# Attention in a diffusion block: ScalarE instead of VectorE makes the rounded high parts of finished pairs and of the keys

## The reference

```python
# latent queries: blocks of 8x16 tokens against a 12x32 neighbourhood and 512 cached tokens
s_lat = einsum(qb, kg) * scale + bias        # relative bias, masked to the 8x16 window
s_ctx = einsum(qb, k_ctx) * scale
p = softmax(concatenate([s_lat, s_ctx], -1))
o = p[..., :n_lat] @ vg + p[..., n_lat:] @ v_ctx
# context queries: blocks of 128 against the 256 context keys
mix = concatenate([o, pool_mixer(u)], -1) @ w_out
```

## Time and profile before

| | |
|---|---|
| median of 3 runs | 4138.67 us (4134.81 to 4142.27) |
| profiled execution | 4139.76 us, span 4138.2 us |
| TensorE busy | 3860.6 us (93%) |
| VectorE busy | 2504.6 us (61%) |
| ScalarE busy | 1815.9 us (44%) |
| GpSimd busy | 502.6 us (12%) |
| from 1120 to 1688 us (attention) | TensorE 523.35, VectorE 392.47, ScalarE 364.50, GpSimd 276.73 of 568 us |

### The profile page before, as it was taken

The page is one execution under the profiler, slowest core; times in us unless marked ns, Lnnn a source line. Parts: engine busy times, 40 slices in busy tenths (PEclk is TensorE's granted clock), DMA queues, the critical chain, the costliest instruction groups (busy, mean ns, idle before and its releaser), DMA issues. The chain is left out here.

```text
span 4138.2 us, 68556 instructions
## 1 busy us (share of the span) xinstructions
PE 3860.6 (93%) x25046; PEld 3388.2 (82%) x25046; DVE 2504.6 (61%) x4812; ACT 1815.9 (44%) x2830; POOL 502.6 (12%) x501
## 2 busy tenths in 40 slices
PE   7999999999799989799997699999999999999992
PEld 3688888888688878799996688888888888888881
DVE  4645555555367777322324677777777777777774
ACT  3611111111266666211104466666666666666652
POOL 0000000000255554000000000000000000000000
PEclk9999999999899999899998799999999999999996
DMA  9434444444555544736316577778777777788776
GB/s 348 152 127 132 137 129 132 132 132 132 151 155 175 159 144 148 252 120 212 128 59 252 168 250 258 255 251 263 252 251 249 252 255 252 257 260 268 250 239 243
DMA packets 572379, 825.46 MB, mean 199 GB/s; under 512 B 23728, under 2 KB 458368, under 8 KB 560512
## 3 DMA queue, kind: packets, MB, share of 16 engines
q1 hardware_dynamic: 548448, 700.96, 52.0%
q0 software_dynamic: 23840, 123.26, 9.2%
HBM read 717.21 MB, written 108.00 MB: 199 GB/s over the span
## 5 line engine op out<-in xcount | busy, mean ns | idle before, releaser
L1959 DVE TENSOR_TENSOR e_wlo<-e_raw,e_whi 128x1024 fp32r<-128x1024 f32 x768 | 905.2, 1219 | 348.9 <-ACT e_whi L1879 345.9
L2091 PE MATMUL ps<-e_xs,e_whi 128*128 128x320 f32 x4096 | 1060.6, 345 | 15.5 <-DVE e_xs L1967 7.9
L2091 PE MATMUL ps<-e_xs,e_wlo 128*128 128x160 f32 x4096 | 934.7, 238 | 0.0
L1879 ACT ACTIVATE e_whi<-e_raw 128x1024 fp32r<-128x1024 f32 x768 | 768.9, 1054 | 326.5 <-DMA e_raw<-in_w_up 109.8
L2091 PEld LDWEIGHTS ps<-e_xs,e_whi 128*128 128x128 f32 x4096 | 754.7, 188 | 24.6 <-DVE e_wlo L1959 11.9
L2091 PEld LDWEIGHTS ps<-e_xs,e_wlo 128*128 128x128 f32 x4096 | 770.3, 191 | 0.7
L2109 PE MATMUL ps<-e_whi,e_h 128*128 128x512 f32 x1024 | 406.2, 397 | 9.2 <-DVE e_h L1993 9.2
L488 PE MATMUL ps<-hhi,p_whi 128*128 128x512 f32 (+1 forms) x1536 | 386.4, 360 | 8.7 <-DVE p_wlo L427 8.7
L445 DVE SCALAR_TENSOR_TENSOR p_acc<-p_modraw,cT,p_acc 128x256 f32<-128x256 f32 x960 | 386.5, 479 | 0.6 <-DMA p_modraw<-in_w_mod 0.6
L488 PE MATMUL ps<-hlo,p_whi 128*128 128x512 f32 (+1 forms) x1536 | 383.4, 358 | 0.0
L488 PE MATMUL ps<-hhi,p_wlo 128*128 128x512 f32 (+1 forms) x1536 | 383.1, 358 | 0.0
(11 more groups left out here) (245 smaller groups left out, 5708.7 us busy)
## 6 DMA issues: line engine op xcount, KB each, us to landing
e_raw<-in_w_gate SPq DMA_DIRECT2D x64, 2048.0 KB
e_raw<-in_w_up SPq DMA_DIRECT2D x64, 2048.0 KB
e_raw<-in_w_down SPq DMA_DIRECT2D x64, 2048.0 KB
p_modraw<-in_w_mod SPq DMA_DIRECT2D x128, 512.0 KB, 3.6
m_raw<-in_w_mod SPq DMA_DIRECT2D x16, 2048.0 KB, 14.8
p_raw<-in_w_in SPq DMA_DIRECT2D x64, 512.0 KB, 4.9
o_raw<-in_w_out SPq DMA_DIRECT2D x16, 2048.0 KB, 8.6
projT<-p_out_st POOLq DMA_DIRECT2D x32, 640.0 KB, 3.7
```

The costliest lines, as they stand in the source:

```text
L1879: nc.scalar.activation(piece(whi, c, q), piece(raw, c, q), ACT.Copy).then_inc(w_hi_made, 1)
L1959: nc.vector.tensor_tensor(piece(wlo, c, q), piece(raw, c, q), piece(whi, c, q).bitcast(F32), ALU.subtract).then_inc(w_lo_made, 1)
L2091: last = nc.tensor.matmul(bank[:, 0:cols], w[:, s, at:at + P], xs[:, k, 0:cols], start=(k == 0 and w is whi), stop=(k == KD - 1 and w is whi))
```

## The change

The copies that make high parts move from VectorE to ScalarE. In `split_pair` the cast to `athi` goes, and ScalarE's new `pair_high(j, w)` makes it, right behind `exps(u+3)`; VectorE then waits for `out_hi`, made by ScalarE, ahead of the subtraction. `k_high` moves too: the first to the head of ScalarE's list, `k_high(j, 1)` to u = 2, and `k_high(j+1, 0)` to u = 13 (it was at u = 12 on VectorE), behind `pair_high`. GpSimd's `make_lo` waits for it as before. `q_low`, the subtractions and all other steps stay.

```diff
@@ ScalarE
+            def pair_high(j, w):
+                if w < W - 1:
+                    act.wait_ge(copied, j * U + (FIRST_PAIR + w + 1))
+                else:
+                    act.wait_ge(pair_copied, j + 1 + AHEAD)
+                if w == 0:
+                    act.wait_ge(att_stored, j * 32 + AHEAD)
+                nc.scalar.activation(tokens_of(athi, w), as_tokens(prT[:, (FIRST_PAIR + w) % 2, NKEY:1024], w), ACT.Copy
+                                     ).then_inc(out_hi, 1)
+            def k_high(j, h, units):
+                act.wait_ge(kq_in, j * 192 + (96 * h + 96))
+                act.wait_ge(scored, units)
+                nc.scalar.activation(khh[:, h, :], kraw[:], ACT.Copy).then_inc(k_hi_made, 1)
+            k_high(0, 0, 0)
             scale_q(0, 0)
...
                     if not last or u + 3 < U:
                         exps(j, u + 3)
+                    if pair_with(u + 1) is not None:
+                        pair_high(j, pair_with(u + 1))
...
                         q_high(j, 1, j * U + 1)
+                    if u == 2:
+                        k_high(j, 1, j * U + 1)
+                    if u == 13 and not last:
+                        k_high(j + 1, 0, j * U + W)
...
                 copy_last_pair(j)
+                pair_high(j, W - 1)
@@ VectorE
             def split_pair(j, w):
-                if w < W - 1:
-                    dve.wait_ge(copied, j * U + (FIRST_PAIR + w + 1))
-                else:
-                    dve.wait_ge(pair_copied, j + 1 + AHEAD)
-                if w == 0:
-                    dve.wait_ge(att_stored, j * 32 + AHEAD)
+                dve.wait_ge(out_hi, j * W + (w + 1))
                 both = as_tokens(prT[:, (FIRST_PAIR + w) % 2, NKEY:1024], w)
-                nc.vector.tensor_copy(tokens_of(athi, w), both).then_inc(out_hi, 1)
-                dve.wait_ge(out_hi, j * W + (w + 1))
                 nc.vector.tensor_tensor(tokens_of(atlo, w), both, tokens_of(athi, w).bitcast(F32), ALU.subtract
                                         ).then_inc(out_lo, 1)
-            def k_high(j, h, units):
-                dve.wait_ge(kq_in, j * 192 + (96 * h + 96))
-                dve.wait_ge(scored, units)
-                nc.vector.tensor_copy(khh[:, h, :], kraw[:]).then_inc(k_hi_made, 1)
-            k_high(0, 0, 0)
             q_low(0, 0)
...
-                    if u == 2:
-                        k_high(j, 1, j * U + 1)
...
-                    if u == 12 and not last:
-                        k_high(j + 1, 0, j * U + W)
```

## The result

| | before | after |
|---|---|---|
| median of all timed runs | 4135.24 us (22 runs, 4119.19 to 4144.42) | 4144.29 us (22 runs, 4136.88 to 4155.91) |
| ratio after / before, 95% interval | | 1.0028 [1.0018, 1.0037] |
| profiled execution | 4139.76 us, span 4138.2 us | 4145.65 us, span 4144.1 us |

A forecast was written before the change was run, and what follows sets the result against it. TensorE was taken to bound about fifty of 68 us of a body. Terms -3.8 - 9.5 - 1.8 - 0.7 + 0.6 + 0.1 = -15.1 us gave 4124 us, 0.35% faster; range 4112 to 4176.

The forecast's parts named there:

- (4): End of a loop body: pair_high(8) ahead of the last copy adds 0.16 us; the later bias adds 0 to 0.3, hidden.
- (1): VectorE's loop work: dropping two 1.08 us key casts and ten athi casts a body is worth 0 in TensorE-bound stretches.
- (2): ScalarE's loop work: k_high takes 1.71 us, pair copies 0.17 each; 4.9 us more a body, covered, so 0.
- (3): Hot stretch after exps(15): GpSimd's run starts 3.4 us later, output(15) comes 0.70 us sooner, a 2.4 us TensorE hole stays.
- the -0.54 a body: Usual loop body: 0.70 us won by output(15), 0.16 lost at the body's end; -3.8 us over seven bodies.
- Missed switch: Rival in the hot stretch: atlo(3) loses one GpSimd switch, 1.1 us later; +4.3 us in all, 4132 us; chance 0.14.
- starved subtraction: Rival: atlo held until GpSimd's run ends if arriving 0.1 us or less before a switch; every body, 4174 us; chance 0.22.
- Clock too: Rival: the mid-body hole shrinks enough that its slow-clock stretch goes, 12 us more gained, 4112 us; chance 0.04.
- (5): Odd long bodies: the 9.22 us cast goes, -9.5 us; the 2.46 us subtraction shortens, -1.8; a like one, -0.7.
- the -1.8: The 70.70 us body: its 2.46 us subtraction would arrive before a GpSimd switch, winning 1.8 of 2.3 us.
- The -0.7: The body at 1584: a collision like the 2.46 us subtraction would shorten, an estimated 0.7 us.
- (6): Loop start: the first stats wait for the bias behind a 1.71 us key copy instead of 1.09, +0.6; end +0.1.

The follow-up runs named there:

- experiment 4: The changed kernel plus seven identity transposes on TensorE ahead of its wait for a body's last pair; 0.9991 of the kernel before.
- experiment 1: The changed kernel with k_high back on VectorE and only pair_high on ScalarE; 1.0011 of the kernel before, median 4147.39 us.
- experiment 2: The changed kernel with the pair casts back on VectorE and only k_high on ScalarE; 0.9988 of the kernel before.
- experiment 3: The changed kernel with pair_high ahead of the exponential in ScalarE's list instead of behind it; 0.9991 of the kernel before.
- experiment 6: The changed kernel with k_high(j+1, 0) at u = 12 ahead of q_high instead of at u = 13; 1.0018 of the kernel before.
- experiment 5: The changed kernel with pair_high ahead of the exponential and k_high back on VectorE; 0.9977 of the kernel before.
- experiment 10: The kernel before, with GpSimd waiting for its window-mean stores to land before its next key subtraction; 0.9985 of the kernel before.
- experiment 7: The kernel before plus twenty identity transposes on TensorE in the 2.4 us hole before unit 15's output; 0.9973 of the kernel before.
- experiment 11: The kernel before, with GpSimd's window-mean stores held back so that its run always follows them without a pause; 1.0093 of the kernel before.
- experiment 9: The changed kernel with pair_high ahead of exps, k_high on VectorE, and GpSimd waiting for its stores to land; 0.9944 of the kernel before, median 4116.73 us.

## Why the prediction was wrong

**The step that failed is (4), "The body's end", with its "+0.16 a body" and, for the later bias, "0 to +0.3, hidden by ScalarE's copy of unit 18".** It goes with the zeros of (1) and (2), where I priced what happens in TensorE-bound stretches at nothing, and with "I leave the slow clock where it is" in (3). Output(19) comes 1263.25 - 1249.60 = 13.65 us after output(15), instead of about 12.9 before. That +0.77 is made of things I had each called hidden: the waits of about 0.98 us for `athi`, the 0.98 us for the bias, and the collision at pair 6 (1.04 instead of 0.29). It lengthens TensorE's hole by 0.74. As a delay alone this would still have been small. What I had no step for is the second stretch at the lower clock: 7.20 x 0.47 = +3.4 us a body. Experiment 4 shows it by itself, since with the hole filled and all waits kept the body is back at 68.5 us. In experiments 1, 2, 3 and 6, each of which leaves out or moves one part, that stretch is gone as well. None of the signs that I had named for being wrong came up in the usual bodies (an `atlo` of over 2.5 us, a late q_low, waits that go over to `prT`): they all belonged to ways of failing that I had thought of. That the pair-6 collision comes from the 3.44 us shift of GpSimd's run is read from the timelines, not tested apart from the bias wait.

**(1) and (2), costs of the moved work: right in size.** The key copy takes 1.69 to 1.73 us (said 1.71). ScalarE's 4.9 us a body are covered, as experiment 3 shows.

**(3), the hot stretch: right, nearly to the tenth.** Relative to `exps(15)`, whose rows are

```profile
1236.76 1.00 ACT L864 ACTIVATE pr<-ps,a_st 128x896 f32<-128x896 f32 x1
...
1241.37 1.69 ACT L937 ACTIVATE khh<-kraw 128x1792 fp32r<-128x1792 f32 x1
```

on ScalarE and

```profile
1243.13 5.72 POOL L771 TENSOR_TENSOR kll<-kraw,khh 128x448 fp32r<-128x448 f32 x4 [6.48 <-ACT khh L937]
```

on GpSimd, the run starts 6.37 us later, where it was 2.93 before: +3.44 (said 3.4). `atlo(3)` starts 8.43 us behind (said 8.40) and takes 0.34, so it won its switch. Output(15) comes 12.84 us behind, before 13.44: -0.60 (said -0.70). "VectorE's gain is thus given back to a wait for ScalarE" held (1.62 us), and the hole of 2.26 stayed. The forecast of this stretch was right, but the -0.54 a body that I made of it did not come: -0.60 here and +0.77 at the end leave +0.17, and in experiment 4, where the clock doesn't fall at the end, a usual body is 68.54 us against 68.37.

**The rivals.** *Missed switch* and *starved subtraction* did not occur in the change's profiled bodies. But the argument against the second, "the only starved instruction was a cast, never a subtraction", was no safe one: in experiments 1, 5 and 6 subtractions were held for 8.80 to 9.56 us. And its condition was wrong: not the phase, but a run of GpSimd right behind its stores (needed in every case seen, but not enough in one); in the change the key copy is late enough that GpSimd has waited before it (6.48 us in the row above). *Clock too* had the right mechanism with the wrong sign: I asked only whether the known slow stretch might go, not whether another hole might make a second.

**(5), the odd bodies: -9.5 us is right for the profiled pair and too much for the median.** The held cast is gone, and by the experiments because of that idle time of GpSimd rather than because the cast was removed. In an average run of the kernel before, all such events less what the pause costs are worth what experiment 10 gains, 0.15% or 6 us. For the body of 70.70 us I had misread the cause. It is longer mainly because its slow stretch lasts 7.00 us and not 4.20, behind the same hole of 2.41 us:

```profile
1384.50:1391.50 7.00, 7.00 (x33) 6.70 (x33) 4.86 (x13) 2.85 (x7) 5.98 (x7) 0.51 0.91 191
```

7.00 x 0.49 less 4.20 x 0.41 is 1.7 of the 2.3 us, which leaves 0.6 for the subtraction of 2.46 us. In experiment 7, which has no slow stretch there, that body is 0.7 us over its neighbours, with a cast of 1.98 us. So the -1.8 stood for a stretch of the clock and not for a collision. In experiment 4 this body takes 68.52 us like the others. No test singled out the -0.7.

**(6), the start: +3.0 instead of +0.6.** The +0.6 itself was right: the first stats come 13.26 us behind the first key copy (1101.10 to 1114.36), before 12.62. But from the first key copy to `q_low(0, 1)` it is 38.2 us (1101.10 to 1139.29), before 35.2. The other 2.4 us again go with the clock: TensorE, busy throughout, has a granted clock of 0.50 from 1123 to 1128, where in the kernel before it is at 0.99 from 1125 on. That is read from the windows, not tested. In addition that `q_low` met a run behind stores:

```profile
1136.60 1.11 POOL L826 DMA_DIRECT2D window_mean_less_u<-pd  x2 [0.30 <-POOL pd L821]
```

```profile
1139.29 4.22 DVE L1025 TENSOR_TENSOR qst<-q,qst 64x1280 fp32r<-64x1280 f32 x1
```

**The account.** From the first `q_low(j, 1)` to the last of the attention loop the profiled executions took 491.1 us before and 497.6 after, +6.5: the new slow stretches, less the held cast. With +3.0 at the head and +0.4 at the tail (to the last subtraction) that is +9.9; the stage began 2.7 us sooner and the rest of the kernel gave 1.3, which leaves the +5.9 of the spans (4138.2 to 4144.1). The medians differ by more, 11.6 us by the ratio; the profiled execution of before had a held cast of 9.22 us, more than the 6 us of an average run, which explains some 3 of the missing 6. The rest stays open; the median of the kernel before moved by more than that from one set of runs to the next (4135.24 to 4142.5).

## What to carry to other kernels

Price a hole of TensorE by its length and by the granted clock behind it: read the clock in windows behind each hole, since holes of one length were followed by a fall in some bodies and not in others, and when a change makes any engine a little later than a TensorE transpose needs, ask whether a hole grows that was harmless so far. A small copy that another engine waits for belongs ahead of a long instruction in its queue, not behind it: moving `pair_high` ahead of `exps` was worth 0.37% against the change, with no other edit. When an instruction now and then lasts until another engine's whole run is over, look at what that engine did just ahead of the run, and try a wait for its own stores there; then read what the later start of its run does to the holes.

## What the runs showed of the hardware

- A granted clock of about half followed holes of 1.28 us (7.20 us at 0.53) and of 2.26 to 2.40 us (3.60 us at 0.55, 4.20 at 0.59) in an otherwise busy TensorE, and did not follow holes of 0.54 and 1.01 us in this kernel. Length alone doesn't decide: no fall followed holes of 1.90 and 2.27 us in the changed kernel's last body of the loop, of 1.64 us and twice of 2.3 in experiment 2, and three times of 2.19 us in experiment 3. And one length, 2.41 us, was followed by 4.20 us at 0.59 or by 7.00 at 0.51. Filling a hole with transposes of the identity removed the slow stretch behind it: at the body's end in experiment 4 (72 matmuls in 8.00 us instead of 36 in 7.20), in its middle in experiment 7 (36 in 4.20 us instead of 22).
- A VectorE cast or subtraction can be held by GpSimd's two-input instructions for a whole run of up to ten, 8.80 to 10.26 us. It happened in seven of seven bodies when the run followed GpSimd's own issue of stores without a pause (experiment 11), and in none of seven when it waited for the stores to land (experiments 9 and 10). In one body of experiment 5 the run followed without a pause and the subtraction took 0.87 us only. Why the issue has this effect, and why it had none there, isn't shown.
- ScalarE copies 128x1792 fp32 within SBUF in 1.69 to 1.73 us, where VectorE's cast took 1.08.
